# State-space layer: two heads on the two column halves take the three matmuls of their outputs in turn

## The reference, cut to what matters

```python
seg = cs_t[..., :, None] - cs_t[..., None, :]
decay_in = jnp.exp(jnp.where(tril, seg, -jnp.inf))
cb = jnp.einsum("bclgn,bcsgn->bcgls", cc, bc)
y_diag = jnp.einsum("bcgls,bcghls,bcsghp->bclghp", cb, decay_in, xdt)
...
y_off = jnp.einsum("bclgn,bcghpn,bclgh->bclghp", cc, prev, jnp.exp(cs))
return (y_diag + y_off).reshape(bsz, Lp, SSD_HEADS, SSD_HEADDIM)
```

## Time and the profile before

| what | value |
| --- | --- |
| median of three runs | 1461.5 us (1461.16 to 1461.75) |
| the profiled execution, own time | 1462.19 us |
| its span in the profile | 1460.4 us |
| mean granted TensorE clock | 0.987 |
| PE busy | 1399.4 us, 96% of the span |
| DVE busy / ACT busy / POOL busy | 72% / 57% / 35% |
| the chain that ended last | PE 76%, DVE 13%, ACT 7% |
| line 1397 and line 1399, all of them | 64 passes each, median 312 ns |
| line 1398, all of them | 64 passes, median 214 ns |

### The profile page before, as it was taken

The page is one execution under the profiler, slowest core; times in us unless marked ns, Lnnn a source line. Parts: engine busy times, 40 slices in busy tenths (PEclk is TensorE's granted clock), DMA queues, the critical chain, the costliest instruction groups (busy, mean ns, idle before and its releaser), DMA issues.

```text
span 1460.4 us, 29915 instructions
## 1 busy us (share of the span) xinstructions
PE 1399.4 (96%) x12819; PEld 1178.7 (81%) x12819; DVE 1053.6 (72%) x1361; ACT 832.3 (57%) x1253; POOL 518.2 (35%) x420
## 2 busy tenths in 40 slices
PE   5999999999999999999999999999899999999997
PEld 3878888887778888878678788887777778788886
DVE  3888986557797885558686888766767774898853
ACT  4566544336674544446885656544576767576651
POOL 0123896112145991225210465401212112146620
PEclk9989999999989999999999999999999999999999
DMA  8443466554333665534336365553434233556550
GB/s 332 170 145 116 145 213 210 187 190 149 115 115 116 229 205 202 198 103 163 115 114 233 117 202 187 174 194 107 151 113 141 76 114 116 202 179 205 192 177 29
DMA packets 35700, 235.21 MB, mean 161 GB/s; under 512 B 4720, under 2 KB 6768, under 8 KB 8816
## 3 DMA queue, kind: packets, MB, share of 16 engines
q1 hardware_dynamic: 35568, 233.31, 46.7%
HBM read 232.24 MB, written 1.05 MB: 160 GB/s over the span
## 4 chain that ended last, share of the span: by engine, by line
PE 76%; DVE 13%; ACT 7%; issue 2%; DMA 1%; SPq 1%; DVEq 0%; ACTq 0%
PE psum L689 23%; PE psum L690 23%; PE psum L691 23%; DVE low L2102 4%; PE psum L777 2%; DVE arena L2492 2%; ACT high L1500 2%; DMA raw<-stream 1%; ACT m L1850 1%; DVE m L2560 1%; PE psum L1009 1%; DVE arena L2563 1%; PE psum L992 1%; ACT arena L1987 0%; ACT L1984 0%
## 5 line engine op out<-in xcount | busy, mean ns | idle before, releaser
L2102 DVE SCALAR_TENSOR_TENSOR low<-raw,high 128x2048 f16<-128x2048 f32 (+4 forms) x246 | 525.8, 2143 | 259.5 <-ACT high L1500 259.3
L689 PE MATMUL psum<-u,high 128*128 128x256 f16 (+4 forms) x2168 | 599.8, 277 | 26.7 <-DVE low L2102 15.4
L690 PE MATMUL psum<-u,high 128*128 128x256 f16 (+4 forms) x2168 | 598.9, 276 | 0.0
L691 PE MATMUL psum<-u,low 128*128 128x256 f16 (+4 forms) x2168 | 598.9, 276 | 0.0
L1500 ACT ACTIVATE high<-raw 128x2048 f16<-128x2048 f32 (+4 forms) x246 | 419.1, 1709 | 136.5 <-PE psum L691 126.3
L689 PE MATMUL psum<-arena,high 128*128 128x256 f16 (+2 forms) x1264 | 346.7, 274 | 2.8 <-ACT arena L1835 1.5
L690 PE MATMUL psum<-arena,high 128*128 128x256 f16 (+2 forms) x1264 | 346.6, 274 | 0.0
L691 PE MATMUL psum<-arena,low 128*128 128x256 f16 (+2 forms) x1264 | 346.6, 274 | 0.0
L689 PEld LDWEIGHTS psum<-u,high 128*128 128x128 f16 (+2 forms) x2168 | 213.0, 98 | 71.6 <-issue 21.7
L690 PEld LDWEIGHTS psum<-u,high 128*128 128x128 f16 (+2 forms) x2168 | 213.3, 98 | 31.6 <-issue 0.7
L691 PEld LDWEIGHTS psum<-u,low 128*128 128x128 f16 (+2 forms) x2168 | 213.3, 98 | 31.2
(11 more groups left out here) (324 smaller groups left out, 1468.6 us busy)
## 6 DMA issues: line engine op xcount, KB each, us to landing
raw<-stream SPq DMA_DIRECT2D x208, 1024.0 KB, 4.9
raw<-stream SPq DMA_DIRECT2D x8, 768.0 KB, 4.1
con<-consts SPq DMA_DIRECT2D x1, 1758.0 KB, 12.4
raw<-stream SPq DMA_DIRECT2D x3, 512.0 KB, 3.6
raw<-stream SPq DMA_DIRECT2D x2, 712.0 KB, 5.6
h<-x_t SPq DMA_DIRECT2D x1, 1024.0 KB, 5.7
out_t<-h SPq DMA_DIRECT2D x4, 256.0 KB, 2.4
raw<-stream SPq DMA_DIRECT2D x1, 896.0 KB, 5.5
```

The source lines that it names most:

```text
L689: pe.matmul(out, w_hi, x[0], start=start, stop=False)
L690: pe.matmul(out, w_hi, x[1], start=False, stop=False)
L691: return pe.matmul(out, w_lo, x[0], start=False, stop=stop)
L2102: tell(dve.scalar_tensor_tensor(low[:, at:at + w], raw[:, off:off + w], W_SCALE, high[:, at:at + w], ALU.mult, ALU.subtract), split_ready ...
```

## The change

Before, a head took its three matmuls one after the other, and then came the next head. Now the heads are taken in the pairs (0, 1) and (2, 3), and the two heads of a pair take each of the three in turn: 1397 of both, 1398 of both, 1399 of both. Number, shapes, operands and places of the matmuls are the same; so are the waits. The increment still hangs on the last matmul, that of head 3.

```diff
-                    for h in range(4):
-                        at, heads = (h // 2) * REST, slice(h * HD, h * HD + HD)
-                        pe.matmul(bank(6, at, at + REST, half_rows(h)), xdt[:, heads], seg[:, h, :], start=True, stop=False)
-                        pe.matmul(bank(6, at + P, at + REST, half_rows(h)), xdt_c[0:META, heads], seg_c[0:META, h, :], start=False, stop=False)
-                        mm = pe.matmul(bank(6, at, at + REST, half_rows(h)), prev[:, heads], cd[:, h, :], start=False, stop=True)
+                    for pair in ((0, 1), (2, 3)):
+                        at = (pair[0] // 2) * REST
+                        for h in pair:
+                            pe.matmul(bank(6, at, at + REST, half_rows(h)), xdt[:, h * HD:h * HD + HD], seg[:, h, :], start=True, stop=False)
+                        for h in pair:
+                            pe.matmul(bank(6, at + P, at + REST, half_rows(h)), xdt_c[0:META, h * HD:h * HD + HD], seg_c[0:META, h, :],
+                                      start=False, stop=False)
+                        for h in pair:
+                            mm = pe.matmul(bank(6, at, at + REST, half_rows(h)), prev[:, h * HD:h * HD + HD], cd[:, h, :], start=False, stop=True)
                     mm.then_inc(y_done, 1)
```

## The result

The changed kernel takes 1465.8 us (median of 13 runs, 1464.0 to 1467.8), the kernel before beside it 1461.6 us (13 runs, 1460.6 to 1464.3). The ratio is 1.0026, with an interval of 1.0017 to 1.0034. That is 4.2 us slower, above the range that was forecast, and it is the fourth rival, the clock, that came true, in all three groups that it names. The profiled execution of the changed kernel took 1465.35 us, its span is 1463.6 us (before: 1462.19 and 1460.4).

The account below looks back on a forecast made before the run. TensorE was taken to carry three quarters of the chain, with waits on other engines swallowing most calls' savings. Groups 4, 6 and 7 give 0.15 + 0.95 + 0.36 = 1.46 us, from 1461.5 to 1460.0 us; range 1457.8 to 1462.6.

Parts of the forecast that it names:

- the fourth rival, the clock: Longer `last_inputs` waits, groups 1 to 3, drop TensorE's clock: 1.7 us a fall; chance 0.12, shared with other POOL-VectorE clashes.
- the last rival, on the clock: Clock falls behind `last_inputs` waits, groups 1 to 3: one gives 1461.7, three 1465.1 us; chance 0.12, shared with other clashes.
- The call: One call of `second_outputs` goes from nine stretches to five, 2.82 to 1.87 us, saving 0.95 us.
- Eight calls, three in the chain: Of eight `second_outputs` calls, only those of groups 4, 6 and 7 count; the others' savings only lengthen waits.
- Clock: Waits at `last_inputs`, groups 1 to 3, grow to 2.2 and twice 2.05 us; each fall costs 1.7; shared chance 0.12.
- Group 4: TensorE reaches `last_inputs(5)` 0.61 us earlier, but of the call's 0.95 us only 0.15 is left.
- the clash: In group 5, POOL's 2934 lies across VectorE's `low_y`, which takes 1.90 us in place of 0.69: +1.2 us.
- Groups 6 and 7: Group 6's call keeps all 0.95 us; group 7's keeps 0.36, the rest becoming a wait for bank 2 at `out_m`.

Follow-up runs that it names:

- e1: Changed kernel with pairs only in groups 3 to 7, head by head in groups 0 to 2; 1461.0 us against 1461.7 for the kernel before.
- e2: Changed kernel with pairs only in groups 0, 1 and 2, head by head elsewhere; 1467.1 us, ratio 1.0029 to the kernel before.
- e8: e3 with group 4's call head by head again; run once for its profile: 40.26 us between the waits in groups 4 and 6, changed kernel 40.09.
- e6: e3 with the bank waits of `out_m` moved to each tile's first matmul; 1459.7 us against 1461.9 for the kernel before.
- e3: Changed kernel plus nine filler matmuls ahead of the wait in `last_inputs` of groups 1, 2 and 3; 1460.3 us against 1461.7 for the kernel before.
- e10: Kernel before with only heads 0 and 1 paired, in groups 0 to 2; 1466.8 us, ratio 1.0029 to the kernel before.
- e11: e3 with six filler matmuls in place of nine; median 1463.2 us, ratio 1.0009 to the kernel before.
- e7: e6 plus fourteen filler matmuls ahead of the wait in `last_inputs(0)`; 1459.0 us against 1461.9 for the kernel before.
- e5: e3 with three filler matmuls in place of nine; 1466.7 us, ratio 1.0032 to the kernel before.

## Why the prediction was wrong

**The step that failed** is the one under the last rival, on the clock: "The waits of 1.27 and 1.1 us in groups 1 to 3, behind which it stayed at the upper level, become 2.2 and twice 2.05." The lengths were right (2.21, 2.06, 2.06), the price was right, and the place in the chain was right. What failed is that the forecast counted as if the clock stayed up behind them too, for which it had no row. The trace of before had one case with a fall (2.75 us) and three without (1.27 and less), and 2.05 to 2.2 lies nearer to 2.75. The price should have entered the sum, and "three give 1465.1" was the forecast to make: measured were 1465.8 in the median and 1465.35 in the profiled execution. The range stopped at one fall, although one cause acted on all three waits alike: they were no three independent mishaps. What the forecast could not know is that its one case with a fall, the wait in group 0, passes without one in five of twelve later profiles.

Point by point:

- *The call*, 1.87 us forecast: 1.88. The two 16-row heads side by side at 0.22 and the long stretch at 0.65 (0.64) were both as taken. The Trainium skill's page "TensorE: Matmul & The Clock Gate", section "The mechanism", speaks of weight loads alone (they overlap running matmuls only where the row groups differ); that pairing would then hide nothing was the prediction's own conclusion from it. That doesn't come true here: two heads with the same 16 rows take, loads included, the 0.22 us that one did. The 0.13 us is the fixed part of a stretch, worked out from two rows; no run shows how much of it is the emptying of the array.
- *Eight calls, three in the chain*: right. The saving of the groups 0 to 2 went wholly into the waits behind them, and that is where it did harm.
- *Clock*: forecast in the rival at 1.7 us a fall. From the wait at 1072.34 to 1099.86 it is 27.52 us, and in e1, from 1074.88 to 1100.72, without a fall, 25.84: 1.68 a fall. Three make 5.0, and e2 shows the same 5 alone (1467.1 against 1461.7, 5.4).
- *Group 4*, 0.15 forecast with the clash: 0.17. TensorE came to `last_inputs(5)` 0.60 us earlier, 0.61 was forecast, and e8 shows that the clash comes with the pair. The wait at `second_inputs(5)` was to be 1.2 us and is 1.02.
- *Groups 6 and 7*, 0.95 + 0.36 = 1.31: 1.24. The handover from ScalarE's last copy to `out_m` took 0.20 us (ACT's 1490 ended at 1222.56) and not 0.14. e6 shows that the wait was for the bank.
- Without the fall the forecast holds: e3 is all that was forecast and lies 1.4 us under before, where 1.46 was the sum.

The account closes: 5.0 lost behind three waits, 0.16 and 1.24 won, 3.6 us; the medians are 4.2 apart. The other 0.6 is within what single executions differ by: the profiled one of before lay 0.6 us over its median, that of the changed kernel 0.4 under. The stretch in group 0, in which the kernels don't differ, comes and goes by itself. Other half-speed stretches, between 84 and 99 us and between 394 and 419, differ in length from execution to execution too.

What stays open: which of the waits between 1.4 and 1.7 us bring a fall. The profiles have two falls in six cases, and the two falls followed the longest; the same kernel comes out on several levels from run to run (e10, e11). Nor was it found why the wait of 2.74 us in group 0 passed without a fall in five of twelve profiles. Something beside the length of a wait counts there, its moment perhaps; that was not tested.

## What to carry to other kernels

A wait of TensorE that another engine ends is no free buffer for savings ahead of it: shortened work makes the wait longer, and behind a longer wait TensorE can fall to half speed, on the chain (here behind all three that grew from 1.1 or 1.27 us to over 2). So before shortening work ahead of such a wait, read its present length and what the clock did behind waits of the new length; if there is no row for it, put the fall into the sum at every such wait together, since one cause moves them all. Dummy matmuls in the idle time cost nothing where TensorE would have waited anyway, and enough of them kept the clock up (nine here, in all twelve waits profiled in e3, e6, e7 and e8; three did not). Then even a saving off the chain is harmless.

## What the runs showed of the hardware that was not expected

- A standstill of 1.73 us or more was followed by half speed in 13 of 13 cases of the groups 1 to 3 (in group 0, 2.74 us, in 7 of 12), and one of 1.07 to 1.27 us in none of 25. In the changed kernel the fall shows 1.5 us after TensorE is back (1072.34 to 1073.82) and lasts until 1077.20, 3.4 us, which costs 1.68 us, more than the whole saving of a call. In the other cases of the groups 1 to 3 it shows 0.4 (e2) to 1.9 us (e5) after TensorE is back.
- Nine filler matmuls ahead of each of the three waits took 5.5 us off the changed kernel's median (1465.8 to 1460.3); three took nothing off (1466.7).
- Two float32 matmuls of 16 rows and 64 columns each, on the two column halves, take 0.22 us from start to start, the same as one.
- A VectorE subtraction of 516 columns with two SBUF inputs takes 0.69 us where GpSimd's multiplication starts only as it ends, and 1.90 where that starts 0.2 us ahead of it.
